# Linear attention of a two-layer block: both pairs' scores between quarters of a gate tile, and one product with the sum of both directions' masked scores

## The chip, the core and the metric

One core of a Trainium2 chip runs the kernel. Its engines work side by side, each through its own instruction stream in order: TensorE (matmuls; PE in the profile), VectorE (DVE), ScalarE (ACT), GpSimd (POOL), and SyncE (SP), which issues the DMAs. They meet by semaphores. TensorE writes only to PSUM, here eight banks of 128 x 512 float32; SBUF holds the operands. The metric is the device time of one execution in microseconds, median of several runs.

## The reference, cut to what matters

The reference is a whole block of mixers; the change touches only its gated linear attention (GLA). It has 4 heads with keys of 64 and values of 128 channels, 768 positions (256 of context, 512 of the sequence) in chunks of 64, and it is run in two directions, whose outputs are added:

```python
def step(s, inp):
    qi, ki, vi, bi = inp                      # one chunk; bi: running sum of the log gates
    diff = bi[:, :, :, None, :] - bi[:, :, None, :, :]
    dec = jnp.exp(jnp.where(causal[:, :, None], diff, -jnp.inf))
    att = jnp.einsum('bhtd,bhsd,bhtsd->bhts', qi, ki, dec)
    o = jnp.einsum('bhtd,bhde->bhte', qi * jnp.exp(bi), s) + jnp.einsum('bhts,bhse->bhte', att, vi)
    bl = bi[:, :, -1:, :]
    s_new = s * jnp.exp(bl[:, :, 0, :])[..., None] + jnp.einsum('bhsd,bhse->bhde', ki * jnp.exp(bl - bi), vi)
    return s_new, o
...
oa_f, sa_f = gla_chunked(aq, ak, av, alog[:, :, 0], sa_f)
oa_b, sa_b = gla_chunked(rev(aq), rev(ak), rev(av), rev(alog[:, :, 1]), sa_b)
return oa_f + rev(oa_b), ...
```

A second projection of the input, the gate `ag`, goes through silu and multiplies the normed output later.

## The kernel before

The heads are taken in two pairs, `hp` = 0 and 1; both heads h of a pair lie side by side in the 128 partitions, and both directions n are computed for a pair together. All matmuls are float32. The 512 positions of the sequence are four row tiles `a` of 128 (two chunks each). For a pair, the steps are:

1. `gla_queries`, `gla_keys`: VectorE subtracts running sums, ScalarE takes the exponential, VectorE multiplies. `gla_keys` has eight regions, (n, j), and for each a subtraction (L835), an exponential on ScalarE (L959) and a product (L826).
2. `gla_ends`: decayed keys (L845, ScalarE's exponential L964, L848), turned by TensorE with 12 transposes in four groups (L673), copied out of PSUM by ScalarE (L970) into `KN`.
3. `gla_sums`: 44 small matmuls, keys by values, one for each chunk, head and direction, into banks 0 to 5.
4. `gla_states`: VectorE chains the sums to states, 2 copies (L864) and 20 steps (L866), and so frees banks 0 to 5.
5. `gla_scores`: for each row tile a 32 matmuls of 64x64 on 16 columns, into a pair of banks for two row tiles.
6. `gla_out_v`: VectorE multiplies the scores with the masks of both directions (L884), two instructions for each a, one for each half of the rows, into `AT`, which has two buffers (a % 2), each with a part for each direction.
7. `gla_out_t`: for each a 8 matmuls, queries by states, in quarters of the array, and 4 full ones, `AT` by values, one for each head and direction, all adding up in a pair of banks; ScalarE copies the sum out (L977).

The four tiles of the projection `ag` (`gate_tile`, 8 matmuls of 128x128 on 512 columns each) are filler. Every order is written out by hand, in one function for each engine: `gla_t` (TensorE), `gla_v` (VectorE), `gla_a` (ScalarE), `gla_g` (GpSimd) and `gla_s` (SyncE). In TensorE's order after the six value tiles come: the first pair's sums, gate tile 0, the second pair's turned keys, the first pair's four scores, its four output tiles, the second pair's sums, gate tiles 1 and 2, then four times a quarter of gate tile 3 (two of its 8 matmuls) and a score of the second pair, and its output tiles. At the end all engines meet, and the norm of the output and the next projection begin.

Semaphores are counts: each engine has one, `nt["sc", hp, k]` is the value of TensorE's when that step is done, and a wait covers all that the engine did before. `Banks.take` waits until the last user of a bank has been copied out (`ps.empty`), before the first matmul is issued into it; `take_two` does it for a pair of banks. `Lane.do` makes an engine wait for its own last instruction. All matmuls go through the helper `mm` and so show as L147.

Of the kernel before, what the change touches and what calls it, by code (L numbers as in the profile page):

```python
# [7 lines left out]
ACT = mybir.ActivationFunctionType  # L8
# [104 lines left out]
def program(nc, I, out):  # L113
# [472 lines left out]
    AT = rmf[:, 512:1536].rearrange("p (b a h n) -> p b a h n", b=2, a=2, h=2)  # L586
# [20 lines left out]
    def gla_t(t):  # L607
# [27 lines left out]
        for a in range(6):  # L635
            p = ps.take(t, "av", a)
            projN(t, p, w, 0, 512, a, ("av", a))
            if a == 2:
                gla_ends_t(t, 0)
# [3 lines left out]
        def gate_tile(a, lo=0, hi=8):  # L643
            p = ps.banks[(6, 6, 7, 0)[a]] if lo else ps.take(t, "ag", a, bank=(6, 6, 7, 0)[a])
# [6 lines left out]
        gate_tile(0)  # L651
        gla_ends_t(t, 1, (7, 0, 1, 2))
        for a in range(4):
            gla_scores_t(t, 0, a, (6, 0))
        gla_out_t(t, 0, (2, 4))
        gla_sums_t(t, 1)
        gate_tile(1)
        gate_tile(2)
        for a in range(4):
            gate_tile(3, 2 * a, 2 * a + 2)  # L660
            gla_scores_t(t, 1, a, (6, 2))
        nt.mark("weights", 3)
        gla_out_t(t, 1, (4, 0))
# [3 lines left out]
    def gla_ends_t(t, hp, banks=(None,) * 4):  # L667
        for n in range(2):
            t.wait_ge(sv, nv["kd", hp, n])
            for a0, a1 in ((0, 4), (4, 6)):  # L670
                p = ps.take(t, "kn", hp, n, a0, bank=banks[2 * n + a0 // 4])
                for a in range(a0, a1):
                    x = t.go.transpose(p[:, 128 * (a - a0):128 * (a - a0) + 128], E[:, n, 128 * a:128 * a + 128], ident)  # L673
                x.then_inc(st, nt("kn", hp, n, a0))
# [48 lines left out]
    def gla_out_t(t, hp, banks):  # L723
        for a in range(4):
# [9 lines left out]
            for h in range(2):  # L734
                for n in range(2):
                    x = mm(t.go, p[:, h, 0:128], AT[:, a % 2, n, h, :],
                           av[:, 2 + a, 128 * (2 * hp + h):128 * (2 * hp + h) + 128], False, n == 1)
# [134 lines left out]
    def gla_out_v(v, hp):  # L872
        v.wait_ge(sg, ng["between"])
        m = cst[:, C_INC:C_INC + 128].rearrange("p (n q) -> p n q", n=2).unsqueeze(2)
        for a in range(4):
            v.wait_ge(st, nt["sc", hp, a // 2])
            if a >= 2:
                v.wait_ge(st, nt["oa", hp, a - 2])
            elif hp:
# [3 lines left out]
            for r in (slice(0, 64), slice(64, 128)):  # L883
                v.do.tensor_tensor(AT[r, a % 2, :, :, r], sc[r], m[r].to_broadcast([64, 2, 2, 64]), ALU.mult).then_inc(sv, nv("at_", hp, a))  # L884
# [3 lines left out]
    def gla_a(a_):  # L888
# [39 lines left out]
        for n in range(2):  # L928
# [2295 lines left out]
```

## Time and profile before

| what | value |
|---|---|
| median of 3 runs | 1347.65 us (1347.24 to 1349.14) |
| the profiled execution, own time | 1348.67 us |
| its span, first to last instruction | 1346.9 us |
| TensorE busy | 1297.1 us, 96% of the span |
| VectorE, ScalarE, GpSimd busy | 678.5, 411.7, 384.9 us |
| mean granted TensorE clock | 0.996 of full |

Times in the rows are microseconds from the start of the span. Busy time counts instructions that execute; idle time of an engine is put down to the instruction that released it. The clock is what was granted to TensorE, as a share of full speed.

### The profile page before, as it was taken

What the parts mean: (1) busy time and instruction counts of PE and PEld (TensorE: products, weight loads), DVE (VectorE), ACT (ScalarE), POOL (GpSimd) and SP (SyncE); (2) the same over time, 40 slices, a digit from 0 to 9 for tenths busy, and PEclk for the clock granted to TensorE, in tenths of its full rate; (3) what the DMA queues carried; (4) which work ended last, traced back from release to release, by engine and by line L of the source; (5) the groups of instructions that cost most, each with busy time, mean ns of one, the idle gap of its engine ahead of it and who ended that gap; (6) DMA issues with size and microseconds to landing.
All of it is one profiled execution on the core that took longest, in us unless ns stands there. A gap on an engine that the chain in (4) does not pass through costs nothing.

```text
span 1346.9 us, 23813 instructions
## 1 busy us (share of the span) xinstructions
PE 1297.1 (96%) x9587; PEld 788.4 (59%) x9587; DVE 678.5 (50%) x1400; ACT 411.7 (31%) x895; POOL 384.9 (29%) x461
## 2 busy tenths in 40 slices
PE   5999999999999999999999999998999999998997
PEld 3454655555667777778445776445655777445653
DVE  4366647846334344464465363237736363337735
ACT  4243303263432222201014102236613202236621
POOL 0100000212324443154531230127731140127731
PEclk9999999999999999999999999999999999999999
DMA  9710012101320100031254415110003515100001
GB/s 311 270 63 33 32 64 79 49 14 63 108 83 3 65 2 2 3 126 63 93 184 96 132 32 188 63 51 2 1 17 72 152 34 188 63 1 1 2 1 62
DMA packets 71532, 96.54 MB, mean 72 GB/s; under 512 B 27639, under 2 KB 35247, under 8 KB 71422
## 3 DMA queue, kind: packets, MB, share of 16 engines
q1 hardware_dynamic: 71050, 94.76, 20.9%
q8 instruction: 75, 1.23, 0.4%
q14 instruction: 35, 0.29, 0.1%
q10 hardware_dynamic: 372, 0.27, 0.1%
HBM read 92.89 MB, written 2.13 MB: 71 GB/s over the span
## 4 chain that ended last, share of the span: by engine, by line
PE 83%; DVE 5%; SPq 3%; ACT 3%; POOL 2%; issue 2%; DMA 1%; DVEq 0%; POOLq 0%; ACTq 0%
PE PS L147 80%; PE PS L2784 2%; DVE AR L2890 1%; ACT AR L3012 1%; POOL AR L3071 1%; SPq L187 1%; POOL AR L2006 1%; DMA bias_rows<-AR 1%; DMA AR<-in_final_g 1%; SPq L304 1%; SPq L308 0%; SPq L309 0%; ACT AR L3022 0%; SPq L312 0%; DVE AR L2877 0%
## 5 line engine op out<-in xcount | busy, mean ns | idle before, releaser
L147 PE MATMUL PS<-AR 64*64 64x64 f32 (+14 forms) x8950 | 1224.6, 333 | 22.9 <-ACT AR L3022 6.1
L147 PEld LDWEIGHTS PS<-AR 64*64 64x64 f32 (+6 forms) x8950 | 719.1, 155 | 500.2 <-issue 405.5
L3012 ACT ACTIVATE AR<-AR 128x257 f32<-128x257 f32 (+5 forms) x160 | 84.9, 531 | 98.7 <-DVE AR L2890 89.4
L2890 DVE CUSTOM_DVE_ANT_0 AR<-PS,AR 128x257 f32<-128x257 f32 (+5 forms) x160 | 72.3, 452 | 61.2 <-PE PS L147 43.7
L412 POOL TENSOR_TENSOR AR<-AR 128x1 f32<-128x1 f32 (+4 forms) x26 | 21.9, 841 | 262.7 <-DVE AR L407 215.9
L1181 DVE SCALAR_TENSOR_TENSOR AR<-AR 128x441 f32<-128x441 f32 (+2 forms) x96 | 78.6, 819 | 15.7 <-ACT AR L1138 12.0
L1568 DVE TENSOR_TENSOR AR<-PS,AR 128x256 f32<-128x256 f32 x60 | 25.5, 425 | 100.7 <-PE PS L147 97.7
L3071 POOL TENSOR_SCALAR AR<-AR 128x257 f32<-128x257 f32 (+5 forms) x96 | 53.4, 556 | 59.4 <-DVE AR L2896 52.0
L3069 POOL TENSOR_SCALAR AR<-AR 128x128 f32<-128x128 f32 (+3 forms) x64 | 38.9, 608 | 63.4 <-DVE AR L2896 58.2
L1695 ACT ACTIVATE AR<-PS 128x512 f32<-128x512 f32 x48 | 28.7, 597 | 92.5 <-PE PS L147 90.1
L2006 POOL TENSOR_TENSOR AR<-AR 128x512 f32<-128x512 f32 x36 | 47.6, 1323 | 29.1 <-DMA AR<-in_w_o 26.1
L2784 PE MATMUL PS<-AR 128*128 128x128 f32 x352 | 50.0, 279 | 5.5 <-DVE AR L2877 3.4
L2059 DVE TENSOR_TENSOR AR<-PS,AR 128x512 f32<-128x512 f32 x40 | 27.7, 692 | 51.7 <-PE PS L147 50.0
L2784 PEld LDWEIGHTS PS<-AR 128*128 128x128 f32 x352 | 38.6, 141 | 25.6 <-issue 10.7
L1803 POOL TENSOR_TENSOR AR<-AR 128x512 f32<-128x512 f32 x20 | 21.0, 1050 | 84.2 <-PE PS L147 55.6
L3022 ACT ACTIVATE AR<-PS 128x512 f32<-128x512 f32 (+2 forms) x56 | 30.0, 536 | 28.6 <-PE PS L2784 24.7
L2527 DVE SCALAR_TENSOR_TENSOR AR<-AR,PS 128x512 f32<-128x512 f32 x16 | 11.0, 688 | 52.3 <-ACT AR L2532 52.3
L2349 DVE SCALAR_TENSOR_TENSOR AR<-PS,AR 128x256 f32<-128x256 f32 x42 | 17.8, 425 | 30.5 <-PE PS L147 22.4
L2877 DVE COPY AR<-PS 128x512 f32<-128x512 f32 (+2 forms) x48 | 28.9, 602 | 8.1 <-PE PS L2784 6.6
L3079 POOL TENSOR_TENSOR AR<-AR 128x28 f32<-128x28 f32 (+3 forms) x8 | 2.5, 315 | 105.8 <-DVE AR L2906 105.3
L2014 POOL TENSOR_TENSOR AR<-AR 128x512 f32<-128x512 f32 x12 | 16.9, 1406 | 53.3 <-PE PS L147 52.6
L1201 POOL TENSOR_TENSOR AR<-AR 128x512 f32<-128x512 f32 (+1 forms) x12 | 13.0, 1082 | 64.5 <-ACT AR L1147 46.4
(262 smaller groups left out, 956.1 us busy)
## 6 DMA issues: line engine op xcount, KB each, us to landing
AR<-in_w_in SPq DMA_DIRECT2D x16, 2048.0 KB, 8.7
AR<-in_w_mod SPq DMA_DIRECT2D x6, 2048.0 KB, 13.1
AR<-in_w_out SPq DMA_DIRECT2D x4, 2048.0 KB, 12.7
AR<-in_x SPq DMA_DIRECT2D x8, 512.0 KB, 5.4
AR<-in_w_in SPq DMA_DIRECT2D x4, 1024.0 KB, 7.4
AR<-in_w_o SPq DMA_DIRECT2D x2, 2048.0 KB, 8.2
AR<-in_w_in SPq DMA_DIRECT2D x2, 1664.0 KB, 9.1
AR<-in_w_in SPq DMA_DIRECT2D x12, 256.0 KB, 4.2
```

Source lines behind the costliest of these rows:

```text
L147: return t.matmul(o, l, r, start=s, stop=p, skip_group_check=True)
L1181: v.do.scalar_tensor_tensor(out=o_, in0=xi[:, r0 + i - 1:r1 + i - 1, c0 + c - 1:c1 + c - 1], scalar=tap(i, c), in1=o_, op0=ALU.mult, op1=A ...
L1695: a_.do.activation(XX[n], ps.two("xx", n, k_, k)[:, new_at(k):new_at(k) + 512], ACT.Copy, bias=0.0, scale=1.0).then_inc(sa, na("xx", n, k_ ...
L2006: g.do.tensor_tensor(o, x, y, ALU.subtract).then_inc(sg, ng(*name, "T"))
L2059: return v.do.tensor_tensor(o, ps[(*name, p, i)][:, :], x, ALU.add).then_inc(sv, nv(*made))
L2784: x = t.go.transpose(p[:, c + 128 * b:c + 128 * b + 128], PB[j % NJP][e][:, at[b]:at[b] + 128], ident)
L2877: write(dst, src).then_inc(sem, count("pT", l, j, e))
L2890: v.do.tensor_tensor_reduce(PB[j % NJP][e][:, 0:nk], ps["s", l, j, e][:, 0:nk], bias_for(qb, kind, 2 * a + e, nk), 1.0, 3e38, ALU.add, ALU ...
L3012: a_.do.activation(P, P, ACT.Exp, bias=mn[:, j % NJS, e:e + 1], scale=-1.0, accum_out=su[:, j % NJS, e:e + 1]).then_inc(sa, na("p", l, j, e))
L3022: out_of_psum(a_, sa, na, lambda o, x: a_.do.activation(o, x, ACT.Copy, bias=0.0, scale=1.0), l, i - TURN, e)
L3069: x = g.do.tensor_scalar(P, P, r, gt_[:, qb, c:c + 1], ALU.mult, ALU.mult)
L3071: x = g.do.tensor_scalar(P, P, r, one_c, ALU.mult, ALU.mult)
```

## The change

Four things change.

- TensorE: the second pair's turned keys, four groups, each in bank 7, lie between the quarters of gate tile 0. The scores of either pair lie between quarters of a gate tile, the first pair's in tile 1, the second's in tile 3, and in banks 0 to 3. The outputs of both pairs use banks 4 to 7. Gate tile 2 comes after the second pair's sums.
- Masked scores: the products of both directions go to two tiles by one instruction (`AT` and the new `AT2`), and a further VectorE instruction adds them. `AT` has a buffer for each of the four row tiles, so the products no longer wait for output matmuls. GpSimd clears `AT2` as well.
- TensorE multiplies the sum by the values: 2 full matmuls for each row tile, not 4.
- ScalarE: value tile 5 is copied before the second exponential of `gla_ends`; gate tiles 0 and 1 are copied out after the copies of the turned keys; each of the first pair's four output copies is followed by two of the eight key exponentials of the second pair, which used to come after all four copies.

```diff
--- before.py
+++ after.py
@@ -583,7 +583,8 @@
     SH = M(2048).rearrange("p (a c n) -> p a c n", a=2, c=8)
     rmf = rm.rearrange("p a n -> p (a n)")
     SP_ = rmf[:, 0:512].rearrange("p (a k n) -> p a k n", a=2, k=2)
-    AT = rmf[:, 512:1536].rearrange("p (b a h n) -> p b a h n", b=2, a=2, h=2)
+    AT = rmf[:, 512:1536].rearrange("p (a h n) -> p a h n", a=4, h=2)
+    AT2 = M(512).rearrange("p (b h n) -> p b h n", b=2, h=2)
     gate = [up, alrT[:, 0:512], M(512), M(512)]
     last = [63, 0]
     s_up, s_tabs = landing("gla_up"), landing("gdn_tabs")
@@ -636,42 +637,43 @@
             p = ps.take(t, "av", a)
             projN(t, p, w, 0, 512, a, ("av", a))
             if a == 2:
-                gla_ends_t(t, 0)
+                for i in range(4):
+                    gla_ends_t(t, 0, i)
         nt.mark("weights", 2)
         w, = weights(t, 3)
 
         def gate_tile(a, lo=0, hi=8):
-            p = ps.banks[(6, 6, 7, 0)[a]] if lo else ps.take(t, "ag", a, bank=(6, 6, 7, 0)[a])
+            p = ps.banks[6 + a % 2] if lo else ps.take(t, "ag", a, bank=6 + a % 2)
             for t8 in range(lo, hi):
                 x = mm(t.go, p[:, :], hT[:, t8, 128 * a:128 * a + 128], w[:, t8, :], t8 == 0, t8 == 7)
             if hi == 8:
                 x.then_inc(st, nt("ag", a))
 
         gla_sums_t(t, 0)
-        gate_tile(0)
-        gla_ends_t(t, 1, (7, 0, 1, 2))
-        for a in range(4):
-            gla_scores_t(t, 0, a, (6, 0))
-        gla_out_t(t, 0, (2, 4))
-        gla_sums_t(t, 1)
-        gate_tile(1)
-        gate_tile(2)
-        for a in range(4):
-            gate_tile(3, 2 * a, 2 * a + 2)
-            gla_scores_t(t, 1, a, (6, 2))
-        nt.mark("weights", 3)
-        gla_out_t(t, 1, (4, 0))
+        for i in range(4):
+            gate_tile(0, 2 * i, 2 * i + 2)
+            gla_ends_t(t, 1, i, 7)
+        for hp in range(2):
+            if hp:
+                gla_sums_t(t, 1)
+                gate_tile(2)
+            for a in range(4):
+                gate_tile(1 + 2 * hp, 2 * a, 2 * a + 2)
+                gla_scores_t(t, hp, a, (0, 2))
+            if hp:
+                nt.mark("weights", 3)
+            gla_out_t(t, hp, (4, 6))
         ps.ring = list(range(8))
         nt.mark("at", "gla")
 
-    def gla_ends_t(t, hp, banks=(None,) * 4):
-        for n in range(2):
-            t.wait_ge(sv, nv["kd", hp, n])
-            for a0, a1 in ((0, 4), (4, 6)):
-                p = ps.take(t, "kn", hp, n, a0, bank=banks[2 * n + a0 // 4])
-                for a in range(a0, a1):
-                    x = t.go.transpose(p[:, 128 * (a - a0):128 * (a - a0) + 128], E[:, n, 128 * a:128 * a + 128], ident)
-                x.then_inc(st, nt("kn", hp, n, a0))
+    def gla_ends_t(t, hp, i, bank=None):
+
+        n, a0, a1 = i // 2, 4 * (i % 2), 4 + 2 * (i % 2)
+        t.wait_ge(sv, nv["kd", hp, n])
+        p = ps.take(t, "kn", hp, n, a0, bank=bank)
+        for a in range(a0, a1):
+            x = t.go.transpose(p[:, 128 * (a - a0):128 * (a - a0) + 128], E[:, n, 128 * a:128 * a + 128], ident)
+        x.then_inc(st, nt("kn", hp, n, a0))
 
 
 
@@ -732,9 +734,7 @@
                         mm(t.go, p[64 * par:64 * par + 64, h, 0:128], QE[r, hp, n, tk:tk + 64], SH[r, n, 2 * a + par, :], n == 0, False)
             t.wait_ge(sv, nv["at_", hp, a])
             for h in range(2):
-                for n in range(2):
-                    x = mm(t.go, p[:, h, 0:128], AT[:, a % 2, n, h, :],
-                           av[:, 2 + a, 128 * (2 * hp + h):128 * (2 * hp + h) + 128], False, n == 1)
+                x = mm(t.go, p[:, h, 0:128], AT[:, a, h, :], av[:, 2 + a, 128 * (2 * hp + h):128 * (2 * hp + h) + 128], False, True)
             x.then_inc(st, nt("oa", hp, a))
 
     def gla_v(v):
@@ -870,18 +870,20 @@
                     ps.empty(sv, nv, "ds", hp, b)
 
     def gla_out_v(v, hp):
+
         v.wait_ge(sg, ng["between"])
         m = cst[:, C_INC:C_INC + 128].rearrange("p (n q) -> p n q", n=2).unsqueeze(2)
         for a in range(4):
             v.wait_ge(st, nt["sc", hp, a // 2])
-            if a >= 2:
-                v.wait_ge(st, nt["oa", hp, a - 2])
-            elif hp:
+            if hp:
                 v.wait_ge(st, nt["oa", 0, 3])
             sc = ps.two("sc", hp, a // 2).rearrange("p (h x) -> p h x", h=2)[:, :, 128 * (a % 2):128 * (a % 2) + 128]
             sc = sc.rearrange("p h (n q) -> p n h q", n=2)
             for r in (slice(0, 64), slice(64, 128)):
-                v.do.tensor_tensor(AT[r, a % 2, :, :, r], sc[r], m[r].to_broadcast([64, 2, 2, 64]), ALU.mult).then_inc(sv, nv("at_", hp, a))
+                o, o2 = AT[r, a, :, r], AT2[r, a % 2, :, r]
+                both = bass.AP(tensor=o.tensor, offset=o.offset, ap=[list(o.ap[0]), [o2.offset - o.offset, 2], list(o.ap[1]), list(o.ap[2])])
+                v.do.tensor_tensor(both, sc[r], m[r].to_broadcast([64, 2, 2, 64]), ALU.mult).then_inc(sv, nv())
+            v.do.tensor_tensor(AT[:, a], AT[:, a], AT2[:, a % 2], ALU.add).then_inc(sv, nv("at_", hp, a))
             if a % 2:
                 ps.empty(sv, nv, "sc", hp, a // 2)
 
@@ -925,22 +927,26 @@
         gla_keys_a(a_, 0)
         value(3)
         gla_queries_a(a_, 1)
-        for n in range(2):
-            gla_ends_a(a_, 1, n, exp=True)
+        gla_ends_a(a_, 1, 0, exp=True)
         value(5)
-        a_.wait_ge(st, nt["ag", 0])
-        a_.do.activation(gate[0], ps["ag", 0][:, :], ACT.Copy, bias=0.0, scale=1.0).then_inc(sa, na("ag0"))
-        ps.empty(sa, na, "ag", 0)
+        gla_ends_a(a_, 1, 1, exp=True)
         for n in range(2):
             gla_ends_a(a_, 1, n, exp=False)
-        gla_out_a(a_, 0)
-        gla_keys_a(a_, 1)
-        a_.do.activation(gate[0], gate[0], ACT.Silu, bias=0.0, scale=1.0).then_inc(sa, na("ag", 0))
-        for a in range(1, 4):
+        for a in range(2):
+            a_.wait_ge(st, nt["ag", a])
+            a_.do.activation(gate[a], ps["ag", a][:, :], ACT.Copy, bias=0.0, scale=1.0).then_inc(sa, na())
+            ps.empty(sa, na, "ag", a)
+        for a in range(4):
+            gla_out_a(a_, 0, a)
+            gla_keys_a(a_, 1, 2 * a, 2 * a + 2)
+        for a in range(2):
+            a_.do.activation(gate[a], gate[a], ACT.Silu, bias=0.0, scale=1.0).then_inc(sa, na("ag", a))
+        for a in range(2, 4):
             a_.wait_ge(st, nt["ag", a])
             a_.do.activation(gate[a], ps["ag", a][:, :], ACT.Silu, bias=0.0, scale=1.0).then_inc(sa, na("ag", a))
             ps.empty(sa, na, "ag", a)
-        gla_out_a(a_, 1)
+        for a in range(4):
+            gla_out_a(a_, 1, a)
         na.mark("at", "gla")
 
     def gla_queries_a(a_, hp):
@@ -951,12 +957,12 @@
             a_.do.activation(x1, x1, ACT.Exp, bias=0.0, scale=1.0 / 16).then_inc(sa, na("qx1", q))
             a_.do.activation(x2, U[:, q, 256:768], ACT.Exp, bias=0.0, scale=1.0 / 16).then_inc(sa, na("qx2", q))
 
-    def gla_keys_a(a_, hp):
-        for n in range(2):
-            for j in range(4):
-                reg, s0, s1 = key_region(hp, n, j)
-                a_.wait_ge(sv, nv["key", hp, n, j])
-                a_.do.activation(reg, reg, ACT.Exp, bias=0.0, scale=1.0 / 16).then_inc(sa, na("key", hp, n, j))
+    def gla_keys_a(a_, hp, i0=0, i1=8):
+        for i in range(i0, i1):
+            n, j = i // 4, i % 4
+            reg, s0, s1 = key_region(hp, n, j)
+            a_.wait_ge(sv, nv["key", hp, n, j])
+            a_.do.activation(reg, reg, ACT.Exp, bias=0.0, scale=1.0 / 16).then_inc(sa, na("key", hp, n, j))
 
     def gla_ends_a(a_, hp, n, exp):
         if exp:
@@ -971,13 +977,12 @@
                              ACT.Copy, bias=0.0, scale=1.0).then_inc(sa, na("kn", hp, n, a0))
             ps.empty(sa, na, "kn", hp, n, a0)
 
-    def gla_out_a(a_, hp):
-        for a in range(4):
-            a_.wait_ge(st, nt["oa", hp, a])
-            a_.do.activation(oA[:, a, 256 * hp:256 * hp + 256].rearrange("p (h n) -> p h n", h=2),
-                             ps.two("oa", hp, a).rearrange("p (h n) -> p h n", h=2)[:, :, 0:128],
-                             ACT.Copy, bias=0.0, scale=1.0).then_inc(sa, na())
-            ps.empty(sa, na, "oa", hp, a)
+    def gla_out_a(a_, hp, a):
+        a_.wait_ge(st, nt["oa", hp, a])
+        a_.do.activation(oA[:, a, 256 * hp:256 * hp + 256].rearrange("p (h n) -> p h n", h=2),
+                         ps.two("oa", hp, a).rearrange("p (h n) -> p h n", h=2)[:, :, 0:128],
+                         ACT.Copy, bias=0.0, scale=1.0).then_inc(sa, na())
+        ps.empty(sa, na, "oa", hp, a)
 
     def gla_g(g):
         meet(g, "setup")
@@ -987,6 +992,7 @@
         g.do.memset(rm[:, 1, 63:768:64], 0.0).then_inc(sg, ng("rm"))
         g.do.memset(KI, 0.0).then_inc(sg, ng("zero"))
         g.wait_ge(sv, nv["b", 1])
+        g.do.memset(AT2, 0.0).then_inc(sg, ng())
         g.do.memset(AT, 0.0).then_inc(sg, ng("between"))
         ng.mark("at", "gla")
 
```

## Rows read from the trace of the kernel before

**Rows 1.** The page, part 1: busy time, share and instructions of the engines.
```profile
PE 1297.1 (96%) x9587; PEld 788.4 (59%) x9587; DVE 678.5 (50%) x1400; ACT 411.7 (31%) x895; POOL 384.9 (29%) x461
```
**Rows 2.** Timeline of TensorE, 131 to 192 us: start, length, what, idle before and releaser.
```profile
131.87 9.71 PE L147 MATMUL PS<-AR 64*64 64x128 f32 x104 [1.60 <-ACT AR L897]
141.41 1.47 PE L673 MATMUL PS<-AR 128*128 128x128 f32 x12
143.04 3.06 PE L147 MATMUL PS<-AR 64*64 64x16 f32 x194 [0.16 <-ACT AR L970]
147.21 9.29 PE L147 MATMUL PS<-AR 64*64 64x16 f32 x158 [1.10 <-issue]
157.06 34.87 PE L147 MATMUL PS<-AR 64*64 64x128 f32 x488 [0.56 <-ACT AR L977]
```
**Rows 3.** Stretches: length, busy PE, PEld, DVE, ACT, POOL, PEclk, DMA, GB/s.
```profile
149.20:152.50 3.30, 3.30 (x28) 2.75 (x27) 0.84 (x2) 0.38 (x1) 0.00 (x0) 0.50 0.02 5
157.06:159.60 2.54, 2.54 (x88) 2.40 (x88) 1.98 (x4) 1.28 (x4) 0.00 (x0) 1.00 0.00 0
166.70:173.60 6.90, 6.90 (x18) 3.08 (x17) 6.26 (x19) 0.73 (x2) 0.00 (x0) 1.00 0.00 0
173.60:185.40 11.80, 11.80 (x284) 6.78 (x286) 1.97 (x5) 1.19 (x2) 0.00 (x0) 1.00 0.01 3
185.40:191.95 6.55, 6.53 (x96) 5.29 (x88) 1.69 (x4) 1.15 (x3) 0.00 (x0) 1.00 0.87 312
```
**Rows 4.** Groups by form, 143.04 to 148.4 (first row), 185.4 to 191.95 (others).
```profile
L147 PE MATMUL PS<-AR 64*64 64x16 f32 x256 | 4.2, 207 | 1.3 <-issue 1.1 <-ACT AR L970 0.2
...
L147 PE MATMUL PS<-AR 128*128 128x128 f32 x32 | 4.6, 287 | 0.0
L147 PEld LDWEIGHTS PS<-AR 128*128 128x128 f32 x32 | 3.9, 191 | 0.7 <-issue 0.3 <-DVE AR L884 0.3
```
**Rows 5.** Timeline of ScalarE, 130 to 192 us.
```profile
130.20 0.84 ACT L964 ACTIVATE AR<-AR 128x768 f32<-128x768 f32 x1 [2.02 <-DVE AR L845]
131.13 0.60 ACT L897 ACTIVATE AR<-PS 128x512 f32<-128x512 f32 x1
...
156.53 0.38 ACT L977 ACTIVATE AR<-PS 128x256 f32<-128x256 f32 x1 [1.30 <-PE PS L147]
157.01 0.84 ACT L959 ACTIVATE AR<-AR 128x128 f32<-128x128 f32 x2
...
159.54 0.63 ACT L959 ACTIVATE AR<-AR 128x512 f32<-128x512 f32 x1 [0.73 <-DVE AR L835]
161.73 1.25 ACT L959 ACTIVATE AR<-AR 128x512 f32<-128x512 f32 x2 [1.56 <-DVE AR L835]
...
173.67 0.60 ACT L941 ACTIVATE AR<-PS 128x512 f32<-128x512 f32 x1 [6.14 <-PE PS L147]
...
186.90 0.38 ACT L977 ACTIVATE AR<-PS 128x256 f32<-128x256 f32 x1 [2.02 <-PE PS L147]
...
191.96 0.38 ACT L977 ACTIVATE AR<-PS 128x256 f32<-128x256 f32 x1 [1.30 <-PE PS L147]
```
**Rows 6.** Timeline of VectorE, 135 to 174 us.
```profile
135.25 7.63 DVE L866 SCALAR_TENSOR_TENSOR AR<-AR,PS 128x128 f32<-128x128 f32 x20
...
153.16 0.88 DVE L884 TENSOR_TENSOR AR<-PS,AR 64x256 f32<-64x256 f32 x2 [1.73 <-PE PS L147]
154.07 0.76 DVE L835 TENSOR_TENSOR AR<-AR 128x128 f32<-128x128 f32 x2
157.36 0.29 DVE L826 TENSOR_TENSOR AR<-AR 128x128 f32<-128x128 f32 x1 [2.53 <-ACT AR L959]
...
158.35 0.43 DVE L826 TENSOR_TENSOR AR<-AR 128x256 f32<-128x256 f32 x1
...
164.65 0.82 DVE L826 TENSOR_TENSOR AR<-AR 128x256 f32<-128x256 f32 x2
...
166.25 7.63 DVE L866 SCALAR_TENSOR_TENSOR AR<-AR,PS 128x128 f32<-128x128 f32 x20
```

## The prediction, written before the change was run

> **What bounds the kernel.** I read the page first: TensorE is busy for 96% of the span [rows 1], so what counts is which work and which idle time of TensorE a change removes. All edits lie in the linear attention, about 130 to 192 us, so I went to TensorE's timeline there [rows 2], the table of stretches for its clock and for the length of each kind of work [rows 3], and the timelines of ScalarE and VectorE [rows 5, 6], to see who releases what. The reader should see five things.
>
> - TensorE idles 1.60 us before the first pair's sums, released by ScalarE's copy of the last value tile [rows 2]. ScalarE did an exponential first, 130.20 to 131.04, although the values were ready at 131.87 - 1.60 = 130.27 [rows 2, 5].
> - The scores of the first pair run in one dense piece from 143.04, stop for 1.10 us "issue" at 146.10, and go on; behind them the granted clock is 0.50 of full, the lower level of 1.2 GHz, from 149.20 to 152.50 [rows 2, 3]. The scores of the second pair lie between quarters of a gate tile: no such idle, clock 1.00 [rows 3].
> - The scores of the first pair are done by 148.4 (all 256 records of 16 columns [rows 4]), and its four output tiles by 156.53, 8.1 later (start of ScalarE's last copy); the second pair's four are shown done from 186.90 to 191.96, 1.69 apart [rows 5].
> - The second pair's sums wait 0.56 for the last of those copies [rows 2].
> - VectorE's and ScalarE's keys of the second pair (to 165.47) and VectorE's states (from 165.6) have long slack now: the scores that need them begin at about 175 [rows 3, 6].
>
> **The sum, in order of time.** All times are in the frame of the profiled execution.
>
> *Start of the sums.* ScalarE copies value 5 before the second exponential: 130.27 + 0.03 + 0.60 + 0.14 (gaps as around 131.13 to 131.87) = 131.05 instead of 131.87. The displaced exponential ends at about 131.8 and its turned keys are wanted 4 us later: hidden. Gain 0.82.
>
> *Turned keys between quarters of gate tile 0.* The same 11.0 us of work (131.87 to 142.88) [rows 2] now ends at 142.06. The waits inside are hidden: each turned group has 1.73 us of a quarter behind it, and a copy takes at most 0.6. The last group is in bank 7, though, and gate tile 1 wants bank 7 at once: 0.02 + 0.38 + 0.14 = 0.54 of idle, where there was 0.16. Gate tile 1 starts at 142.6; the scores started at 143.04. The interleaving itself I cost at 0, within 0.2 each way: only twelve transposes, 1.47 us in all, change places with quarters.
>
> *Scores between quarters of gate tile 1.* This is what the second pair does already. From gate tile 2 done (173.67) to the first output copy (186.90) is 13.23 us [rows 5]: a gate tile, four scores, one output tile. Starting from work instead of from a finished tile adds about 0.17 for the tail of the array. With the smaller output product (below) the first copy is at 142.6 + 13.4 - 0.5 = 155.5, and the scores are done at T = 154.5 (an output tile behind dense scores shows after 1.5 us, less 0.5). The states of the first pair ended at 142.88 [rows 6] and now end 0.8 earlier; the scores want their banks at 144.3: no wait. The 1.10 us of issue idle and the slow clock go away. In the old order, scores (143.04 to about 148.45, 5.4) and gate tile 1 (6.9) made 12.3 us; now 11.9.
>
> *Output product.* Each output tile loses two of four matmuls of 128x128 on 128 columns. Each fp32 matmul leaves two records. Four tiles show 32 loads of 128x128 in 3.9 us and as many matmul records, 0.122 us a load [rows 4]. Four records fewer are 0.49 us a tile, 1.96 for four. From below, the pace of the gate tile (6.90 us for 16 records of 512 columns [rows 3], so 0.108 for 128) gives 0.43; from above, (1.69 - 0.48) / 4 for a product gives 0.60 for two, with 0.48 as 16 of the 88 records in 2.54 us of the sums [rows 3]. I take 0.49 because it is this very instruction. The Trainium skill (TensorE: Matmul & The Clock Gate, "LDWEIGHTS (loading the stationary operand)") gives the columns divided by 1.2 in ns, 107 ns for 128 columns; by it the four tiles would save 1.71 instead of 1.96, and the row, 15% above the rule, is used.
>
> *VectorE behind the scores.* Each a now costs two masked products, 0.88 the pair [rows 6] (still 64x256 out of PSUM; that one half lands in another tile I cost at nothing, up to a doubling, see below), and one sum of 128x256 at 0.43 [rows 6]: 1.35 with gaps. Four row buffers make the wait for the output matmuls disappear. For a = 2 and 3 it runs T to T + 2.75; the outputs want it at T + 1.6 and T + 4: no stall there. But only then does VectorE begin the second pair's keys.
>
> *The new stall.* ScalarE's order is now: output copy 0, key exponentials 0 and 1, output copy 1, exponentials 2 and 3, and so on. The copies of tiles that are long finished wait behind exponentials that wait for VectorE. From its first subtraction, the multiply of region 0 follows after 0.8 [rows 6]; exponential 1 ends 0.49, exponential 3 ends 2.81, exponential 5 ends 5.62 after that multiply's start (157.85, 160.17 and 162.98 against 157.36) [rows 5, 6]. So the output copies begin at T + 3.55 + these = T + 4.04, 6.36 and 9.17; each frees its banks 0.52 later.
>  - Output tile 3 takes banks 6 and 7 of tile 1: T + 4.56 instead of T + 3.2, 1.35 idle.
>  - The second sums take banks 4 and 5 of tile 2: T + 6.88 instead of about T + 5.7, 1.2 idle.
>  - Gate tile 2 takes bank 6 of tile 3: T + 9.69, the sums ending at about T + 9.4.
> So gate tile 2 starts at T + 9.65 = 164.15. For the first pair this swallows the clock, the smaller product and the vanished 0.56 together: scores done to sums was 148.45 to 157.06 = 8.6, and becomes 6.88.
>
> *To the end.* Gate tile 2 done: 164.15 + 6.94 + 0.17 = 171.26. From there to the last output copy was 191.96 - 173.67 = 18.29, now 18.29 - 1.96 = 16.33: 187.6 instead of 191.96. ScalarE has nothing between the second pair's copies, so they don't stall. VectorE must free banks 0 and 1 before the scores at T + 18.4: keys end at T + 11.7 (8.11 after the first multiply), and the thirteenth of 20 state steps of 0.38 ends at T + 17.4 [rows 6]: 1.0 us in time. That margin is thin, and it is the next to bind. GpSimd's extra memset lies some 40 us ahead of its reader. Nothing of SyncE moves but the release of the gate weights, which comes earlier.
>
> **Sum: 191.96 - 187.6 = 4.4 us less.** In parts: start of the sums -0.8, bank 7 +0.4, scores and gate tile -0.4, scores to second sums -1.7, wait before gate tile 2 +0.2, second pair's product -2.0. Behind 192 us TensorE is as full as before, so the 4.4 us should reach the end. The profiled execution took 1348.67 (span 1346.9), which would become 1344.3; it is 1.0 above the median of 1347.65, from which one gets 1343.3. Between them: 1343.7 us.
>
> **Rivals.**
> - *Copies not held (11%).* If ScalarE's copies got out before the exponentials, the outputs and sums would take T + 7.2, but the scores would then wait for VectorE's banks at T + 17.5: 0.9 better than T + 18.4, a gain of 5.3, 1342.8 us. Against it: the order is written out.
> - *The clock falls again (17%).* T + 3.2 to T + 6.9 holds about 2.5 us idle, broken by one tile, just as 1.1 us idle came before the old fall. A stretch like the old one cost 8.1 us for four tiles where the second pair's took 6.7, so 1.4: gain 3.0, 1345.1 us. Against it: 1.60 idle before 131.87 had no fall behind it.
> - *The masked product into two tiles is slow (8%).* Doubled to 0.84, VectorE's chain begins its keys 1.7 later, and all of TensorE's waits behind it follow: gain 2.7, 1345.4 us.
> - *The smaller product is worth half (9%),* because the switch between tiled and full matmuls, not the loads, sets 1.69: gain 3.4, 1344.7 us.
> - *Slower (4%).* The clock, once down in those idle stretches, stays down through the sums and gate tile 2, 9.4 us of full-speed work that takes as long again: 9.4 - 4.4 = 5.0 lost, 1353 us. It decides once more than 4.4 us of work is done at half rate; the old stretch ended after 3.3 [rows 3].
>
> **Numbers.** The forecast has 51%. About 0.2%, 2.7 us, is what a measurement of this kernel can tell from no change, so faster means under 1345.0. The forecast and the first rival lie there nearly whole, the others with a half or less: faster 0.66, same 0.30, slower 0.04. Range: from the first rival on the lower basis to the slow product on the upper, 1341.7 to 1346.3.
>
> **What the new profile would show.** Sums at 131.05; clock 1.00 from 140 to 190; no issue idle among the first scores; ScalarE's L977-type copies of the first pair spread over some 8 us between exponentials; TensorE idle about 1.3 and 1.2 us before the last output tile and the second sums, released by ScalarE; output tiles of the second pair 1.2 apart; last copy near 187.6. Wrong would be: a clock of 0.50 behind the idle stretches; scores of the second pair waiting for VectorE; tiles still 1.5 or more apart.

## The result, and the profile after

The changed kernel takes 1344.26 us, median of 9 runs (1343.74 to 1345.51). The kernel before, timed beside it, takes 1348.43 (9 runs, 1346.69 to 1349.98). The ratio is 0.997, 95% interval 0.9961 to 0.9978, so 3.0 to 5.3 us less. The forecast was 1343.7 in a range of 1341.7 to 1346.3.

The profiled execution took 1344.26 us too, with a span of 1342.4. What follows the last output copy (L977 before, L982 now) differs by 0.4 us between the two profiles: 1346.9 - 191.96 = 1154.9 and 1342.4 - 187.84 = 1154.6 us. So most of the 4.5 us between the spans lies in the stretch that was argued about.

TensorE's timeline of the changed kernel (start, length, what, idle before and releaser), to be held against [rows 2]:

```profile
130.90 4.55 PE L147 MATMUL PS<-AR 64*64 64x128 f32 x92 [0.78 <-ACT AR L899]
135.28 0.60 PE L675 MATMUL PS<-AR 128*128 128x128 f32 x4
...
142.39 15.54 PE L147 MATMUL PS<-AR 128*128 128x512 f32 x332 [0.47 <-ACT AR L976]
158.88 1.31 PE L147 MATMUL PS<-AR 64*64 64x128 f32 x20 [0.96 <-ACT AR L982]
161.33 2.64 PE L147 MATMUL PS<-AR 64*64 64x128 f32 x88 [1.14 <-ACT AR L982]
164.16 23.64 PE L147 MATMUL PS<-AR 128*128 128x512 f32 x368 [0.19 <-ACT AR L982]
188.27 7.15 PE L147 MATMUL PS<-AR 128*128 128x512 f32 x16 [0.47 <-ACT AR L982]
```

The granted clock over these 50 us (columns as in [rows 3]; the 1.00 is the clock):

```profile
140.00:190.00 50.00, 46.77 (x818) 27.99 (x818) 29.04 (x68) 12.82 (x25) 0.00 (x0) 1.00 0.13 44
```

The idle before the sums is halved (1.60 to 0.78), the 1.10 of issue idle (time in which TensorE waited for nothing that the profile shows) is gone, the wait after the turned keys is 0.47 where it was 0.16, and three new waits have come, all released by ScalarE's output copies: 0.96 before output tile 3, 1.14 before the second sums, 0.19 before gate tile 2. What those copies stood behind is in ScalarE's timeline (L965 are the key exponentials, L982 the output copies):

```profile
157.47 0.89 ACT L965 ACTIVATE AR<-AR 128x128 f32<-128x128 f32 x2 [1.60 <-DVE AR L835]
158.45 0.39 ACT L982 ACTIVATE AR<-PS 128x256 f32<-128x256 f32 x1
158.92 0.53 ACT L965 ACTIVATE AR<-AR 128x384 f32<-128x384 f32 x1
160.18 0.63 ACT L965 ACTIVATE AR<-AR 128x512 f32<-128x512 f32 x1 [0.72 <-DVE AR L835]
160.90 0.38 ACT L982 ACTIVATE AR<-PS 128x256 f32<-128x256 f32 x1
162.37 1.26 ACT L965 ACTIVATE AR<-AR 128x512 f32<-128x512 f32 x2 [1.08 <-DVE AR L835]
163.72 0.38 ACT L982 ACTIVATE AR<-PS 128x256 f32<-128x256 f32 x1
...
184.12 0.38 ACT L982 ACTIVATE AR<-PS 128x256 f32<-128x256 f32 x1 [1.58 <-PE PS L147]
...
187.84 0.38 ACT L982 ACTIVATE AR<-PS 128x256 f32<-128x256 f32 x1 [0.86 <-PE PS L147]
```

ScalarE sits idle before its exponentials, for VectorE (releaser L835), while a finished output tile waits for its copy. What ScalarE waits for is one engine further, in VectorE's timeline (L885 masked products, L886 the new sum, L835 the first key subtractions, L866 the states):

```profile
154.39 0.88 DVE L885 TENSOR_TENSOR AR<-PS,AR 64x256 f32<-64x256 f32 x2 [3.16 <-PE PS L147]
155.31 0.43 DVE L886 TENSOR_TENSOR AR<-AR 128x256 f32<-128x256 f32 x1
155.77 0.88 DVE L885 TENSOR_TENSOR AR<-PS,AR 64x256 f32<-64x256 f32 x2
156.68 0.43 DVE L886 TENSOR_TENSOR AR<-AR 128x256 f32<-128x256 f32 x1
157.14 0.75 DVE L835 TENSOR_TENSOR AR<-AR 128x128 f32<-128x128 f32 x2
...
166.90 7.63 DVE L866 SCALAR_TENSOR_TENSOR AR<-AR,PS 128x128 f32<-128x128 f32 x20
```

And the two forms that answer to [rows 4], for the second pair's four output tiles, half as many records:

```profile
L147 PE MATMUL PS<-AR 128*128 128x128 f32 x16 | 2.8, 300 | 0.0
...
L147 PEld LDWEIGHTS PS<-AR 128*128 128x128 f32 x16 | 2.1, 190 | 0.7 <-issue 0.3 <-DVE AR L886 0.3
```

### The profile page after: what moved, and what is told of

It reads as the page before. It is cut to its first block, busy times and chain, and to the rows that moved or that the text cites. A ratio compares the mean times of both kernels' runs of the same rounds, so it can differ in the third digit from the quotient of the medians.

```text
span 1342.4 us, 23755 instructions
## 1 busy us (share of the span) xinstructions
PE 1292.3 (96%) x9555; PEld 782.8 (58%) x9555; DVE 683.7 (51%) x1408; ACT 412.6 (31%) x896; POOL 386.3 (29%) x462
## 4 chain that ended last, share of the span: by engine, by line
PE 86%; DVE 5%; ACT 2%; SPq 2%; POOL 2%; DMA 1%; issue 1%; DVEq 0%; POOLq 0%; ACTq 0%
PE PS L147 83%; PE PS L2790 2%; DVE AR L2896 1%; ACT AR L3018 1%; DMA AR<-in_w_mod 1%; SPq L187 1%; DMA AR<-in_final_g 1%; POOL AR L3077 1%; DVE AR L2883 0%; POOL AR L3075 0%; ACT AR L3028 0%; SPq L304 0%; POOL AR L2012 0%; PE PS L2123 0%; DVE AR L2065 0%
## 5 line engine op out<-in xcount | busy, mean ns | idle before, releaser
L147 PEld LDWEIGHTS PS<-AR 64*64 64x64 f32 (+5 forms) x8918 | 713.5, 154 | 500.1 <-issue 402.0
```

The lines of the kernel that those rows point to most:

```text
L147: return t.matmul(o, l, r, start=s, stop=p, skip_group_check=True)
```

## The experiments

To compare traces I use one stretch: from the end of the last value tile (start of the first sums less the idle before it) to the start of the last output copy. It is free of what the start of the kernel does. Each stretch is that of one execution, the profiled one. "Clock" says whether the granted clock fell to 0.50 within it. What follows the stretch varies from 1154.2 to 1154.9 us over these profiles (1154.9 and 1154.5 for the kernel before alone). The runs were made in four sets, each ratio against the runs of before in its own set (medians 1348.43, 1348.02, 1348.11 and 1348.57).

| kernel | stretch, us | clock | time, us | ratio to before, 95% |
|---|---|---|---|---|
| before | 191.96 - 130.27 = 61.69 | falls | 1348.43 (9 runs) | |
| before, second profile | 191.33 - 129.95 = 61.38 | falls | 1347.62 (1) | |
| the change | 187.84 - 130.12 = 57.72 | holds | 1344.26 (9) | 0.9970 (0.9961 to 0.9978) |
| the change, again | 189.29 - 130.16 = 59.13 | falls | 1345.01 (6) | 0.9970 (0.9959 to 0.9982) |
| sum alone | 186.66 - 129.87 = 56.79 | holds | 1343.94 (6) | 0.9969 (0.9957 to 0.9980) |
| sum alone, again | 186.70 - 130.24 = 56.46 | holds | 1343.11 (5) | 0.9962 (0.9948 to 0.9975) |
| order alone | 190.16 - 129.27 = 60.89 | holds | 1347.43 (11) | 0.9995 (0.9986 to 1.0004) |
| change, copies first | 186.99 - 130.23 = 56.76 | holds | 1344.98 (11) | 0.9976 (0.9967 to 0.9985) |
| change, bank 0 | 188.12 - 129.93 = 58.19 | falls | 1342.71 (5) | 0.9965 (0.9953 to 0.9978) |
| the same, second profile | 187.78 - 129.53 = 58.25 | falls | 1343.87 (1) | |
| copies, bank 0, GpSimd | 185.10 - 129.52 = 55.58 | holds | 1341.20 (5) | 0.9950 (0.9937 to 0.9962) |
| sum and two small edits | 186.34 - 129.92 = 56.42 | falls | 1341.28 (5) | 0.9947 (0.9933 to 0.9961) |
| as GpSimd, two quarters | 184.15 - 129.98 = 54.17 | holds | 1339.84 (5) | 0.9935 (0.9922 to 0.9947) |

**The sum alone.** The kernel before, with only the sum, four row buffers and two output matmuls fewer for each row tile (the dots leave out the products into two tiles, the matmuls and GpSimd's memset, all as in the change):

```diff
-    AT = rmf[:, 512:1536].rearrange("p (b a h n) -> p b a h n", b=2, a=2, h=2)
+    AT = rmf[:, 512:1536].rearrange("p (a h n) -> p a h n", a=4, h=2)
+    AT2 = M(512).rearrange("p (b h n) -> p b h n", b=2, h=2)
...
+            v.do.tensor_tensor(AT[:, a], AT[:, a], AT2[:, a % 2], ALU.add).then_inc(sv, nv("at_", hp, a))
```

> The kernel before with the summed masked scores alone (four row buffers, AT2, one VectorE sum and two output matmuls fewer for each row tile); every order stays as before. If the smaller product is worth what its records say, an output tile falls from 1.69 to about 1.24 us in both pairs and the kernel is 3.3 to 3.9 us faster than before, nearly all of the change's gain. If the halved product was mostly hidden (the rival that it is worth half), 1.5 to 2 us. The idle of about 1.1 us among the first scores and the clock of 0.50 behind it should still be there.

Measured: 1343.94 us, and in its second run 1343.11. That is the whole gain of the change. TensorE's timeline has the old shape, with the issue idle still there:

```profile
147.03 5.96 PE L147 MATMUL PS<-AR 64*64 64x16 f32 x142 [1.32 <-issue]
153.55 33.08 PE L147 MATMUL PS<-AR 64*64 64x128 f32 x472 [0.56 <-ACT AR L977]
```

The output copies are 1.24 apart in both pairs (the first and the last of each pair's four):

```profile
149.30 0.38 ACT L977 ACTIVATE AR<-PS 128x256 f32<-128x256 f32 x1 [5.16 <-PE PS L147]
...
153.02 0.38 ACT L977 ACTIVATE AR<-PS 128x256 f32<-128x256 f32 x1 [0.86 <-PE PS L147]
...
182.94 0.38 ACT L977 ACTIVATE AR<-PS 128x256 f32<-128x256 f32 x1 [1.57 <-PE PS L147]
...
186.66 0.38 ACT L977 ACTIVATE AR<-PS 128x256 f32<-128x256 f32 x1 [0.86 <-PE PS L147]
```

To price the sum I take the clock's fall (1.4, measured below on the change) and the issue idle off each stretch, as both vary from profile to profile. Before: 61.69 - 1.4 - 1.10 = 59.2 and 61.38 - 1.4 - 0.82 = 59.2. Sum alone: 56.79 - 1.32 = 55.5 and 56.46 - 0.99 = 55.5. The sum is worth 3.7. The fall behind the dense scores can be priced too, from the restart after the issue idle to the first pair's last copy: 153.33 - 145.80 = 7.53 us with the fall (the sum and two small edits, below) and 153.02 - 147.03 = 5.99 here without it, so 1.5. With that the sum is worth 3.6, and eight tiles by 0.45 are 3.6. One expectation failed: the clock held at 1.00 although TensorE idled even longer, 1.32 us, before the same work.

**The order alone.** The changed kernel, with `AT` in two buffers, four output matmuls a tile, and the wait for the output tiles back:

```diff
-            if hp:
+            if a >= 2:
+                v.wait_ge(st, nt["oa", hp, a - 2])
+            elif hp:
                 v.wait_ge(st, nt["oa", 0, 3])
...
-            v.do.tensor_tensor(AT[:, a], AT[:, a], AT2[:, a % 2], ALU.add).then_inc(sv, nv("at_", hp, a))
```

> The changed kernel without the sum (four output matmuls for each row tile, two buffers, the wait for the output matmuls back), with every new order. By the forecast's arithmetic: scores done at 154.5, VectorE's products then wait for output tiles 0 and 1 and its keys start 1.35 later than in the changed kernel, ScalarE's held copies release the second sums at about T + 8.2 and gate tile 2 at T + 11.0: 1.0 us faster than before, within 0.5. If the new order's clock and idle gains came through whole, it would be 3 us or more faster. If the held copies were worse than reckoned, it would be slower than before.

Measured: 1347.43, a ratio whose interval holds 1, and a stretch 0.8 shorter than before (0.5 against its second profile). The three held copies are there without the sum as well, before output tile 3, the sums and gate tile 2:

```profile
159.43 1.76 PE L147 MATMUL PS<-AR 64*64 64x128 f32 x24 [1.01 <-ACT AR L982]
161.88 2.64 PE L147 MATMUL PS<-AR 64*64 64x128 f32 x88 [0.69 <-ACT AR L982]
164.70 25.43 PE L147 MATMUL PS<-AR 128*128 128x512 f32 x384 [0.17 <-ACT AR L982]
```

The order's own gains (0.8 at the start of the sums, the 1.10 of issue idle, 1.4 for the clock when it would fall, the 0.56) add up to 3.9. Of these, 1.9 go back in these three waits, 0.3 in the longer wait before gate tile 1, and some 0.75 because the scores take longer between quarters of a gate tile than in one dense piece (worked out below, at "Scores between quarters"). That leaves some 0.9, near the 0.8 measured.

**Copies first.** The changed kernel with ScalarE's order alone altered:

```diff
-        for a in range(4):
+        for a, i0, i1 in ((0, 0, 0), (1, 0, 2), (2, 2, 3), (3, 3, 8)):
             gla_out_a(a_, 0, a)
-            gla_keys_a(a_, 1, 2 * a, 2 * a + 2)
+            gla_keys_a(a_, 1, i0, i1)
```

> The changed kernel with ScalarE's order changed alone: output copies 0 and 1, key exponentials 0 and 1, copy 2, exponential 2, copy 3, the other exponentials. If ScalarE's held copies make the stalls, the idle of 0.96, 1.14 and 0.19 us before the last output tile, the second sums and gate tile 2 is gone, but the second pair's first scores then wait some 1.7 us for VectorE's states to free banks 0 and 1, and 0.8 to 0.9 us of the 2.3 reach the end. If VectorE does not bind there, 2.3 us reach it. If the copies were not the cause, nothing changes.

Measured in the trace: the three waits are gone, and the predicted one takes their place, before the second pair's scores, released by the states on VectorE:

```profile
142.51 28.13 PE L147 MATMUL PS<-AR 128*128 128x512 f32 x460 [0.47 <-ACT AR L976]
172.09 14.86 PE L147 MATMUL PS<-AR 64*64 64x16 f32 x348 [1.46 <-DVE AR L866]
```

The stretch is 56.76, 0.96 less than the change where the clock held. 2.29 us of waits went and 1.46 came. The median, 1344.98, does not show the 0.96: the intervals of the two ratios overlap, and this difference rests on the trace alone. The eleven times lie in two groups, five at 1342.90 to 1343.64 and six at 1344.98 to 1346.11, and the profiled execution (1343.43) is one of the lower group. What the upper group has in addition, a fall of the clock for instance, no trace shows.

**Bank 0.** The changed kernel, with the last group of turned keys in bank 0:

```diff
-                gla_ends_t(t, 1, i, 7)
+                gla_ends_t(t, 1, i, 0 if i == 3 else 7)
```

> The changed kernel with the last group of the second pair's turned keys in bank 0 instead of 7. If the wait of 0.47 us before gate tile 1 is for the copy out of bank 7, it goes and all that follows comes 0.5 us earlier, to the last output copy at about 187.4. If VectorE's states freed bank 0 late, the wait moves before that group of transposes and nothing is gained.

Measured: gate tile 1 follows the transposes without a wait, and the second sums start 160.41 - 129.93 = 30.48 after the last value tile, against 31.21 in the change. But the stretch is 58.19, because now the clock fell behind the idle of 0.95 and 1.14 us:

```profile
160.41:163.80 3.39, 3.39 (x68) 3.39 (x72) 3.08 (x6) 1.97 (x4) 0.00 (x0) 0.55 0.00 0
```

(Columns as in [rows 3]; the 0.55 is the clock.) The second profile of the same kernel:

> The changed kernel with the last turned group in bank 0, unchanged from its first run, looked at again. In that run the clock fell to 0.50 behind the two idle stretches at 157 to 160 us. If the idle alone decides, it falls again; if it does not fall, the stretch from the last value tile to the last output copy is 57.0 to 57.2 us instead of 58.2.

It fell again, from about 159.8 on, and the stretch was 58.25. The second profile of the change has the fall as well (59.13, below), and against that one bank 0 is 0.9 shorter. The first run's median of 1342.71 us, the lowest up to there, does not contradict the longer stretch: the profiled execution was the slowest of the five, 1344.74, and three others took 1342.50 to 1342.71. That those three had no fall would fit, but they have no trace. What is shown is that the wait of 0.47 goes and that the sums start 0.7 earlier.

**The kernel before, profiled again.**

> The kernel before, unchanged, looked at again. The idle of 1.1 us among the first pair's scores should be there again, since it was there with the sum alone too. Whether the clock falls to 0.50 behind it is open: it did in the profile of before and did not with the sum alone. If the fall belongs to the order of work, it is there again and the stretch from the last value tile to the last output copy is 61.7 us; if not, about 60.3 us.

```profile
146.59 9.27 PE L147 MATMUL PS<-AR 64*64 64x16 f32 x158 [0.82 <-issue]
```
```profile
148.00:151.40 3.40, 3.40 (x32) 2.58 (x25) 0.84 (x2) 0.38 (x1) 0.00 (x0) 0.51 0.02 5
```

It fell again, behind an issue idle of 0.82 us.

**GpSimd's sums.** The change, with copies first, bank 0, and the sums for the first pair's row tiles 2 and 3 moved (TensorE then waits for GpSimd before output tiles 2 and 3):

```diff
...
+            if hp or a < 2:
+                v.do.tensor_tensor(AT[:, a], AT[:, a], AT2[:, a % 2], ALU.add).then_inc(sv, nv("at_", hp, a))
...
+        for a in (2, 3):
+            g.wait_ge(sv, nv["masked", 0, a])
+            g.do.tensor_tensor(AT[:, a], AT[:, a], AT2[:, a % 2], ALU.add).then_inc(sg, ng("at_", 0, a))
```

> The changed kernel with three things more: output copies ahead of the key exponentials, the last turned group in bank 0, and the sums of the first pair's row tiles 2 and 3 on GpSimd (about 0.7 us each, as its other 128x256 operations) instead of VectorE. If VectorE's chain of products, keys and states is what binds once the copies are out of the way, its keys start 0.9 earlier and the wait for the states falls from 1.46 to about 0.6 us. From the end of the last value tile to the last output copy: 57.7 us in the changed kernel, 56.8 with the copies alone, and here 55.2 to 55.5. If GpSimd's sums come too late, a wait before output tiles 2 and 3 takes their place; if VectorE did not bind, only the 0.6 of bank 0 shows.

Measured: 1341.20 us, stretch 55.58. The wait for the states is 1.01, not 0.6. TensorE's, then VectorE's, then GpSimd's rows (in this kernel the key subtractions are L838, the states L869 and the masked products L888):

```profile
170.20 14.86 PE L147 MATMUL PS<-AR 64*64 64x16 f32 x348 [1.01 <-DVE AR L869]
```
```profile
154.88 1.16 DVE L838 TENSOR_TENSOR AR<-AR 128x128 f32<-128x128 f32 x2
```
```profile
154.01 0.73 POOL L1003 TENSOR_TENSOR AR<-AR 128x256 f32<-128x256 f32 x1 [63.23 <-DVE AR L888]
154.93 0.83 POOL L1003 TENSOR_TENSOR AR<-AR 128x256 f32<-128x256 f32 x1 [0.18 <-DVE AR L888]
```

VectorE's first two key subtractions took 1.16 instead of 0.75 us, just while GpSimd's second sum ran (154.93 to 155.76), and that is the missing 0.4. All of it is in the second of the two, which began at about 155.2: 0.83 us instead of 0.43. The first, begun before GpSimd's second sum, took 0.29 in this kernel and in the change.

**The sum and two small edits, without the new order on TensorE.**

```diff
-        for n in range(2):
-            gla_ends_a(a_, 1, n, exp=True)
+        gla_ends_a(a_, 1, 0, exp=True)
         value(5)
+        gla_ends_a(a_, 1, 1, exp=True)
...
-        gla_out_t(t, 0, (2, 4))
+        gla_out_t(t, 0, (4, 6))
```

> The kernel before with the summed masked scores and two small edits, without the new order on TensorE: value tile 5 is copied before the second exponential, and the first pair's outputs lie in banks 4 to 7, so that the second sums don't wait for the last copy. If these waits are independent of the rest, 0.82 and 0.56 us go, and the stretch from the end of the last value tile to the last output copy falls from 56.8 (the sum alone) to 55.4 us, with a further 1.4 on top if the clock falls behind the first scores. Then the new order of TensorE is not needed for the gain. If the dense scores need the new order, it stays at or above 56.8.

Measured: 1341.28 us. Both waits are reduced as expected (1.60 to 0.78, and 0.56 to nothing). The stretch is 56.42, with a fall of the clock in it, to 0.52 on the mean of 146.3 to 149.7. Less 1.4 and the issue idle of 0.87 it is 54.1, against 55.5 for the sum alone: the 0.82 + 0.56 = 1.4 expected. The times, 1341.28 against 1343.94 and 1343.11, agree.

```profile
145.80 40.50 PE L147 MATMUL PS<-AR 64*64 64x16 f32 x614 [0.87 <-issue]
```
```profile
146.30:149.70 3.40, 3.40 (x74) 2.85 (x70) 2.73 (x7) 0.38 (x1) 0.00 (x0) 0.52 0.02 5
```
```profile
153.33 0.38 ACT L977 ACTIVATE AR<-PS 128x256 f32<-128x256 f32 x1 [0.86 <-PE PS L147]
```

**Two quarters ahead.** As the GpSimd kernel, and:

```diff
-                gate_tile(1 + 2 * hp, 2 * a, 2 * a + 2)
+                lo, hi = ((0, 4), (4, 6), (6, 8), (8, 8))[a] if hp else (2 * a, 2 * a + 2)
+                if lo < hi:
+                    gate_tile(1 + 2 * hp, lo, hi)
```

> The changed kernel with the three edits of x5 and one more: two quarters of gate tile 3 ahead of the second pair's first scores, one ahead of its second, one ahead of its third, none ahead of its fourth. If the 1.01 us that TensorE waited for VectorE's states in x5 is only a matter of what lies ahead of these scores, 1.73 us more of gate work hides it: the wait is gone and the stretch from the last value tile to the last output copy falls from 55.6 to about 54.6 us, 1340.2 us in all. If the last two scores, now dense, bring idle or a fall of the clock behind them, half of it or all comes back.

Measured: 1339.84 us, ratio 0.9935 (0.9922 to 0.9947), the fastest of all. The stretch is 54.17, 1.41 shorter than that of the GpSimd kernel, where the wait alone was 1.01; the 0.4 more is not traced. From gate tile 1 to the end of the output TensorE waits for nobody (the second fence is ScalarE's first output copy):

```profile
141.61 42.50 PE L147 MATMUL PS<-AR 128*128 128x512 f32 x808
184.59 7.58 PE L147 MATMUL PS<-AR 128*128 128x512 f32 x17 [0.47 <-ACT AR L988]
```
```profile
154.60 0.38 ACT L988 ACTIVATE AR<-PS 128x256 f32<-128x256 f32 x1 [1.58 <-PE PS L147]
```

**The change and the sum alone on one chip.**

> The changed kernel itself, unchanged, on the same chip as the sum alone. The stretch should be 57.7 us, or about 59 if the clock falls in its idle stretches at 158 to 161 us. If the new order adds anything to the sum, its time is below that of the sum alone; by the traces so far it is 0 to 1 us above.

> The sum alone, unchanged, on the same chip as the changed kernel. The stretch should be 56.8 us, or about 57.8 if the clock falls behind the first scores, which it did in both profiles of the kernel before and not in the first of this one. If the sum carries the gain, its time is within 1 us of the changed kernel's.

Measured: 1345.01 (6 runs, 0.9959 to 0.9982 of before) and 1343.11 (5 runs, 0.9948 to 0.9975). The medians are 1.9 apart and the intervals overlap, so that the change is slower than its own sum is not proven by times; the profiled stretches say so, one of the change against two of the sum, 57.72 against 56.79 and 56.46 with the clock at 1.00 in each. In this profile of the change the clock fell:

```profile
162.00:165.00 3.00, 3.00 (x64) 3.00 (x60) 2.69 (x6) 1.98 (x4) 0.00 (x0) 0.50 0.00 0
```

and the stretch is 59.13, 1.41 more than in the first.

## Why the prediction was right, point by point

- *Start of the sums.* Said 0.82; the idle fell from 1.60 to 0.78 in every kernel that has the edit. Right.
- *Bank 7.* Said 0.54 where there was 0.16; it was 0.47. Bank 0 took it away: the cause is shown.
- *Scores between quarters.* Said to remove the issue idle and the fall of the clock behind it. The idle went, in all profiles. The fall was put down as certain; it is not. Five profiles have the dense scores: the clock fell in three (before twice, the sum with two small edits) and held in two (the sum alone). So a part of this term is sometimes worth nothing. And the interleaving has a price. From the first score to the first output copy the sum alone takes 149.30 - 142.65 = 6.65 us, 5.33 without its issue idle (5.33 in its second profile too); between quarters it is 154.60 - 141.61 = 12.99 in the kernel with two quarters ahead, which is 6.1 without the 6.9 of the gate tile [rows 3]. So what the interleaving saves is 0.82 to 1.32 of idle less about 0.75. The prediction has this inside its step from 12.3 to 11.9 without naming it.
- *Output product.* Said 0.49 a tile between 0.43 and 0.60; measured 1.69 - 1.24 = 0.45. The Trainium skill's rule that the prediction weighed there (TensorE: Matmul & The Clock Gate, "LDWEIGHTS (loading the stationary operand)"), by which it would be 0.43, came 0.02 from the measurement and the row 0.04. The upper bound of 0.60 took 0.48 for 16 records where its row gives 16/88 of 2.54 = 0.46; that moves it by 0.01. The rival that it is worth half is refuted.
- *Masked product into two tiles.* Said at no extra cost: 0.88 the pair, as before. The sum took 0.43, as said. The rival of a doubled product is refuted.
- *The held copies.* Said at T + 4.04, 6.36 and 9.17. With T = 154.39, the start of VectorE's products, they began at T + 4.06, 6.51 and 9.33, and gate tile 2 started at 164.16 where 164.15 was said (T + 9.69, the last line of that list, would be 164.19). The idle itself was reckoned 1.35 and 1.2 and shows as 0.96 and 1.14; the row shows a matmul busy until its modelled end, which would fit. That these copies cause the waits is shown by the copies-first kernel.
- *VectorE is next to bind, 1.0 us away.* Copies first: TensorE waits 1.46 for L866, and 0.96 of 2.29 comes through; the prediction's rival had 0.9.
- *The clock may fall again, 1.4.* It did in the second profile of the change, and cost 59.13 - 57.72 = 1.41. That was a rival with 17%; it came in one of two profiles of the change and in both of the bank 0 kernel, so it was rated too low. The forecast already counts before's own fall as gained, so each execution of the change with a fall lies 1.4 above it. The median of the second set, 1345.01, lies at this rival's 1345.1. The first set's median, 1344.26, is the profiled execution itself, in which the clock held; how many of the other eight had the fall no trace shows. That the median fell on an execution without it, and so near the forecast, is in part luck.
- *The sum.* Said 187.6 for the last copy, in the frame of before; it was 187.84, and the profile after started its stretch 0.15 earlier. So 4.4 was said and 61.69 - 57.72 = 3.97 measured in the stretch, 4.2 between the medians. More than half of the missing 0.4 lies behind the start of gate tile 2: 187.84 - 164.16 = 23.68 where the sum has 23.4, of which the smaller product explains 0.16. The lower end of the range is said to be the first rival on the lower basis, which is 1347.65 - 5.3 = 1342.3 and not 1341.7, and the upper end 1348.67 - 2.7 = 1346.0 and not 1346.3; the measured time lies inside either way.

What the sum did not say, though its terms hold it: the gain is the smaller product's. It put 2.0 on the second pair's tiles and let the first pair's vanish in the 1.7 of "scores to second sums". The sum alone and the order alone show how it splits: 3.6 to 3.7 for the product; for the order by itself 0.5 to 0.8, and that with the clock's 1.4 counted as its gain; and on top of the sum the order takes 0.9 to 1.3 away, where the clock holds in both. They don't add up because both want the same time: in the new order ScalarE's and VectorE's chain sets when the sums start, and a shorter output can't help there.

What stays open: why the clock falls in one execution and not in another of the same work; why the same scores take about 0.75 us more between quarters; and what the issue idle is (0.82 to 1.32 us in the five profiles that have it, always after record 194 of the dense scores, and absent where quarters of a gate tile lie between). Beyond the second profiles, no run here was made for any of these.

## What to carry to other kernels

When two edits come together, reckon each against the other's new critical chain: here the reduction of work carried all of the gain, and the reordering, good for every idle period that it was aimed at, built a chain of two other engines that gave it back. When copies out of PSUM share an in-order engine with work that waits for a third engine, put each copy at the time when its tile is done, not evenly between. And move filler in front of the step whose operands are late: 1.73 us of gate work removed the 1.01 us of waiting that were left after VectorE had been relieved. When a kernel's times fall into two groups, say which group the profiled execution belongs to before a trace is held against a median.

## What was not expected of the hardware

- VectorE's two subtractions with both inputs in SBUF went from 0.75 to 1.16 us while GpSimd added two SBUF tiles, in both kernels that do so. The Trainium skill (SBUF — State Buffer, "Who interferes with whom") says that a VectorE instruction with two SBUF inputs contends with a GpSimd instruction that reads SBUF, and that the port pair they share is an exclusive lock. These rows agree that the two contend: the subtraction begun while GpSimd's sum ran took 0.83 instead of 0.43 us and ended 0.3 after that sum, while the masked products that ran during GpSimd's first sum, with one input in PSUM, took 0.42 to 0.43 each, as in the change. Of the 0.9 us that two sums fewer took off VectorE, 0.41 came back.
- In six profiles the granted clock fell to 0.50 for some 3.4 us, at a price of 1.4 to 1.5 us: in the dense scores behind an idle of 1.10, 0.82 and 0.87 us (before twice, the sum and two small edits), and behind 0.95 or 0.96 and 1.14 us around output tile 3 (the change's second profile, both of bank 0). It held behind 1.32 and 0.99 us in the same dense scores (the sum alone) and behind 0.96 and 1.14 in the change's first profile.
